# Scores of the second block from the rotated halves: three fp32r passes over 64 rows, in turn of the two row halves

## What is computed

```python
# differential attention: 8 heads, each with two components c of 64 features
q = apply_rope(rms_norm_2(q.reshape(B, S, 8, 2, 64), q_norm), cos, sin)
k = apply_rope(rms_norm_2(k.reshape(B, S, 8, 2, 64), k_norm), cos, sin)
s = einsum('bqhcd,bkhcd->bhcqk', qblk, k) * scale          # causal, query blocks of 128
p = softmax(where(causal, s, NEG_INF))
a = p[:, :, 0] - lam * p[:, :, 1]
o = einsum('bhqk,bkhe->bqhe', a, v)                        # then a norm per head and w_o
# sliding window: 16 query heads of 64 features, 4 key heads, window 128
q = apply_rope(rms_norm_2(q, q_norm), cos, sin)
s = einsum('bnqhgd,bnkhd->bnhgqk', qb, kw) / 8             # 128 queries by 256 keys
m = maximum(max(s), sink); e = exp(s - m)
p = e / (sum(e) + exp(sink - m));  o = einsum('bnhgqk,bnkhd->bnqhgd', p, vw)
```

## Time and profile before

| | |
|---|---|
| median of three runs | 2025.56 us |
| profiled execution: time / span | 2027.33 us / 2025.5 us |
| granted TensorE clock, mean share of full | 0.987 |
| PE busy | 1938.7 us (96%) |
| weight loads (PEld) busy | 1560.5 us (77%) |
| DVE busy | 1222.7 us (60%) |
| ACT busy | 791.4 us (39%) |
| DMAs PR<-TMPR | 144, 128.0 KB by the page |
| DMAs TMP<-TMP | 104 |

### The profile page before, as it was taken

One profiled execution on the slowest core, in us unless ns is written; L12 is line 12 of the kernel. 1 busy time (PEld: TensorE's weight loads), 2 busy tenths in 40 slices (PEclk: granted clock), 3 DMA queues, 4 the chain that ended last, 5 costly groups with the idle time before them and its releaser, 6 DMA issues.

```text
span 2025.5 us, 24525 instructions
## 1 busy us (share of the span) xinstructions
PE 1938.7 (96%) x9230; PEld 1560.5 (77%) x9230; DVE 1222.7 (60%) x2147; ACT 791.4 (39%) x1734; POOL 275.9 (14%) x212
## 2 busy tenths in 40 slices
PE   7999899999999999899979999999989899999999
PEld 5887676788888888666658888888867778888887
DVE  8456986655354466488856535545969875445353
ACT  4444555433232233366643323223357633223231
POOL 3000430111011021011111101101210011101010
PEclk9999999999999999999979999999999999999999
DMA  5232000133323323455423333332353123333322
GB/s 208 70 97 70 1 1 1 53 94 97 102 94 96 102 84 104 116 150 130 119 60 94 102 94 94 103 94 86 104 149 83 27 89 98 94 97 101 94 93 95
DMA packets 62134, 184.41 MB, mean 91 GB/s; under 512 B 9024, under 2 KB 9408, under 8 KB 61760
## 3 DMA queue, kind: packets, MB, share of 16 engines
q1 hardware_dynamic: 62016, 182.83, 30.2%
HBM read 155.01 MB, written 2.10 MB: 78 GB/s over the span
## 4 chain that ended last, share of the span: by engine, by line
PE 77%; DVE 11%; SPq 5%; issue 2%; DMA 2%; ACT 2%; DVEq 0%; ACTq 0%
PE bank L880 22%; PE bank L882 21%; PE bank L881 21%; SPq L792 2%; PE bank L984 2%; DMA TMP<-TMP 2%; SPq L769 2%; PE bank L854 1%; PE bank L1055 1%; PE bank L855 1%; PE bank L856 1%; DVE SM L1654 1%; PE bank L1031 1%; PE bank L1075 1%; DVE WL L1438 1%
## 5 line engine op out<-in xcount | busy, mean ns | idle before, releaser
L1159 ACT ACTIVATE WH<-RAW 128x512 fp32r<-128x512 f32 (+2 forms) x584 | 331.8, 612 | 790.5 <-PE bank L882 725.3
L1438 DVE TENSOR_TENSOR WL<-RAW,WH 128x512 fp32r<-128x512 f32 (+2 forms) x584 | 457.7, 817 | 76.3 <-ACT WH L1159 69.8
L880 PE MATMUL bank<-HH,WH 128*128 128x512 f32 x1056 | 424.7, 402 | 22.5 <-DVE WL L1438 9.9
L880 PE MATMUL bank<-GH,WH 128*128 128x512 f32 x1088 | 435.5, 400 | 7.0 <-DVE GL L1710 4.2
L882 PE MATMUL bank<-GH,WL 128*128 128x512 f32 x1088 | 425.3, 391 | 0.0
L881 PE MATMUL bank<-GL,WH 128*128 128x512 f32 x1088 | 425.0, 391 | 0.0
L882 PE MATMUL bank<-HH,WL 128*128 128x512 f32 x1056 | 413.8, 392 | 0.0
L881 PE MATMUL bank<-HL,WH 128*128 128x512 f32 x1056 | 413.7, 392 | 0.0
L880 PEld LDWEIGHTS bank<-HH,WH 128*128 128x128 f32 x1056 | 200.4, 190 | 69.3 <-DVE WL L1438 9.9
L880 PEld LDWEIGHTS bank<-GH,WH 128*128 128x128 f32 x1088 | 205.8, 189 | 51.2 <-issue 5.9
L882 PEld LDWEIGHTS bank<-GH,WL 128*128 128x128 f32 x1088 | 205.1, 188 | 43.6
(11 more groups left out here) (222 smaller groups left out, 2175.6 us busy)
## 6 DMA issues: line engine op xcount, KB each, us to landing
RAW<-in_wgu SPq DMA_DIRECT2D x132, 512.0 KB, 3.5
RAW<-in_wd SPq DMA_DIRECT2D x48, 512.0 KB, 3.5
PR<-TMPR SPq DMA_DIRECT2D x144, 128.0 KB, 2.3
RAW<-in_wd SPq DMA_DIRECT2D x24, 384.0 KB, 3.1
RAW<-in_da_qk SPq DMA_DIRECT2D x16, 512.0 KB, 3.7
TMP<-TMP SPq DMA_DIRECT2D x104, 64.0 KB, 2.0
RAW<-in_w_inh SPq DMA_DIRECT2D x12, 512.0 KB, 3.5
RAW<-in_w_in SPq DMA_DIRECT2D x8, 512.0 KB, 6.5
```

The lines of the kernel that those rows point to most:

```text
L880: e.matmul(b, w_h, hi[st.x][k], start=(k == 0), stop=False)
L1159: e.activation(whs[s % NW][:, a:b], raw[s % NR][:, a:b], ACT.Copy).then_inc(S["wh"], 1)
L1438: e.tensor_tensor(wls[s % NR][:, a:b], raw[s % NR][:, a:b], whs[s % NW][:, a:b].bitcast(F), ALU.subtract).then_inc(S["wl"], 1)
```

## The change

The stacking DMAs of `qk` and `sq` go (those of `ks` stay, all with eight DMAs, 16 in the two units). The rotated halves are written directly to where the scores read them: queries and keys of differential attention into rings of three buffers `qd`, `kd`, those of `sq` into a ring of two, `qw`. `scores` now makes both components, or both heads of a unit, at once: three passes (high by high, low by high, high by low), each as two matmuls, one over rows 0 to 63 into one bank and one over rows 64 to 127 into another; then the two masks. `rhi` on ACT now waits until the scores that read the buffer are made, which `stk` on SP did before. `qn` and `swp` wait for the rotation by two units back, not for its stacking. The sliding-window steps are numbered anew (`swa`): two heads of a unit in turn per query block, so that an even `sc s n` makes scores n and n+1. In the planner `swp` costs 2400 instead of 1500 and the `stk` of `ks` 4900 instead of 3000.

```diff
+def swa(n):
+    return n // 8 * 2 + n % 2, n // 2 % 4
...
+        old = rope and g >= 2 and (("stk" if 16 <= g - 2 < 18 else "rot"), *ropes[g - 2])
+        o.add("DVE", ("qn", *at), 680, ("rs", *at), st == "in" and ("xcv", 1), old)
...
-        o.add("SP", ("swp", *at), 1500, ("qn", *at), g >= 2 and ("stk", *ropes[g - 2]), lands=1700)
+        o.add("SP", ("swp", *at), 2400, ("qn", *at), old, lands=1900)
         o.add("DVE", ("rot", *at), 1400, ("cs", *at), ("swp", *at))
-        o.add("ACT", ("rhi", *at), 520, ("rot", *at))
+        free = None
+        if st == "qk" and m >= 6:
+            free = ("sc", "d", 4 * (m // 2 - 3) + 3)
+        elif st == "sq" and m >= 2:
+            free = ("sc", "s", 8 * (m - 2) + 6)
+        o.add("ACT", ("rhi", *at), 520, ("rot", *at), free)
         o.add("DVE", ("rlo", *at), 620, ("rhi", *at))
...
-        doubled = st == "ks" or st == "qk" and m % 2
-        o.add("SP", ("stk", *at), 3000 if doubled else 1500, ("rlo", *at), free, lands=1900)
+        if st == "ks":
+            o.add("SP", ("stk", *at), 4900, ("rlo", *at), ("zero",), lands=1900)
...
-            o.add("PE", ("sc", a, i), two * (2 * w // 2 + 90) if a != "n" else 4 * w * 10 // 12 + 500, *after(i),
-                  ("ex", a, i - back) if i >= back else first)
+            if a == "s" and i % 2 == 0:
+                o.add("PE", ("sc", a, i), 3 * (w + 32) * 10 // 24 + 300, *after(i), ("ex", a, i - 2) if i else first)
...
-                e.matmul(b[:, 0:n], lhs, rhs, start=True, stop=False, skip_group_check=True)
-                if rhs_lo is not None:
-                    e.matmul(b[:, 0:n], lhs, rhs_lo, start=False, stop=False, skip_group_check=True)
-                e.matmul(b[:, mcol:n], identb, mask, start=False, stop=True,
-                         skip_group_check=True).then_inc(S["sc"], 1)
+            def scores(s, q, k, mask, mcol, n):
+
+                two = score_bank(s), score_bank(s + 1)
                 p.wait_ge(S["cb"], 16)
+                for t, (x, y) in enumerate(((q[0], k[0]), (q[1], k[0]), (q[0], k[1]))):
+                    for c in range(2):
+                        rows = slice(64 * c, 64 * c + 64)
+                        e.matmul(two[c][:, 0:n], x[rows], y[rows], start=(t == 0), stop=False, skip_group_check=True)
+                for b in two:
+                    e.matmul(b[:, mcol:n], identb, mask, start=False, stop=True,
+                             skip_group_check=True).then_inc(S["sc"], 1)
...
             def rhi(st, m):
                 p.wait_ge(S["nm_q"], NM[st] + m - 6 + 1)
-                e.activation(nat_hi[m % 2], tmp[m % 2], ACT.Copy).then_inc(S["nm_hi"], 1)
+                if st == "qk" and m >= 6:
+                    p.wait_ge(S["sc"], SC["d"] + 8 * (m // 2 - 2))
+                elif st == "sq" and m >= 2:
+                    p.wait_ge(S["sc"], SC["s"] + 8 * (m - 1))
+                e.activation(rotated(st, m)[0], tmp[m % 2], ACT.Copy).then_inc(S["nm_hi"], 1)
```

More of the change, by code:

```diff
@@ L1556, in rlo @@
                 p.wait_ge(S["nm_hi"], g + 1)
[L1557 removed]
+                high, low = rotated(st, m)
+                e.tensor_tensor(low, tmp[m % 2], high.bitcast(F),
                                 ALU.subtract).then_inc(S["nm_lo"], 1)
```

110 lines of the change are left out of this document (48 added, 62 removed).

## The result

The changed kernel takes 1992.87 us (median of 4 runs, 1989.85 to 1995.55); the kernel before 2027.13 (4 runs, 2025.24 to 2029.56). The ratio is 0.9831, 95% interval 0.9814 to 0.9848: 34.3 us faster. The forecast was 2008 with a range of 1995 to 2021.

A forecast was written before the change was run, and what follows sets the result against it. SyncE's queue was taken to lead the chain of waits in differential attention (32.4%). Terms -6.5 - 2 - 7 + 2 + 1 = -12.5 there and -4.5 in the sliding window gave -17 from 2027.33, stated as 2008, range 1995 to 2021.

The forecast's parts named there:

- PE's scores: Both attentions: new pair costs 1.17 us at 512 columns, 0.81 at 128 and 256; charged +2 us and +1.5 us.
- Rival D: Scores on PE: the two row halves stream one behind another, +5 us in total, 2030; chance 0.07.
- The start, -6.5: First scores of differential attention: 3.75 us stack wait, 1.3 of clock and 1.5 of a bank wait go.
- The middle, -2: Differential attention: of VectorE's 16.8 us waits for swaps, 2 us gained, bounds 0 and 8; PE mostly has other work.
- The clock: Differential attention's start: reduced clock after the stall loses 2.6 us at full-speed equivalent, of which 1.3 was counted.
- The end, -7: Last head of differential attention: scores begin earlier without stacking; 7 of 9.4 us taken, bounds 3 and 9.4.
- The sliding window, -4.5: Sliding-window attention: weight load ahead of stacks -3, earlier first scores -3, scores on PE +1.5.
- rival C: The wait only moves: ScalarE's high half waits for late scores, giving most back; 2023, chance 0.10.
- Rival A: VectorE takes SyncE's place as pace-setter in the middle; only -8 us, 2017.5, chance 0.22.
- Rival B: More than forecast: freer queue brings every rotation earlier, PE's mode changes hide; 29.7 us gained, put at 1998, chance 0.16.

The follow-up runs named there:

- The better order alone: The kernel before with only the planner's guesses for swap and stack times corrected, every stack still made: 1998.59 us, ratio 0.986.

## Why the prediction was right and wrong

*PE's scores: right.* A pair with 512 columns between dense passes takes 0.10 to go over (0.33 instead of 0.23 us after the dense pass), 0.99 in the record with masks, and the next dense pass comes 0.09 late: 1.18 against 1.17 forecast. At 256 columns 0.83 to 0.89 against 0.81, at 128 0.77 against 0.81. Long streams on the two row halves do overlap. By the Trainium skill ("TensorEngine Tiling (Array Packing)", Tiling Modes, Key Properties) a change of mode drains TensorE; the trace agrees, with about 0.09 us for each. Rival D is out.

*The start, -6.5: right.* The wait became 0.46 us as forecast. The first scores come 12.6 us earlier, but 26 passes of 512 columns, 5.9 us at 0.2275, now stand behind them instead of ahead, so some 6.7 us are saved. It agrees with PE's idle time up to there, 6.2 before and 0.5 after. The better order alone gives 5.5 of it (71.9 against 77.4, with as many passes ahead).

*The middle, -2: the step that failed.* The prediction had PE with other work in most of VectorE's 16.8 us of waits. In fact PE's transposes wait for softmax weights that VectorE makes behind these rotations. Up to the last pass of the dense block's projection the stage became 17.0 us shorter, and less the start's 6.7 that leaves 10.3 for the middle, where 2 were forecast and another 2 charged for the pairs. PE's idle time in the middle fell from 10.0 to 0.9 us, and the clock, 0.978 there before and 1.000 after, gave about 2.9 (estimate). Both stood in the trace of the kernel before: PE's own idle time in the stretch prices the term, VectorE's waits do not.

*The clock: 1.3 in the sum, at the start alone.* By the estimate it is 8.5 of the 35.4 us between the profiled executions: 6.8 in the dense stage, above all at its end, and 5.1 in the sliding window, less 3.4 in the rest.

*The end, -7: 11.6.* Between the last projection pass and the last head's norm the stage takes 34.9 instead of 46.5 us: 4.9 less idle time, about 4.2 of clock, the rest not assigned. The better order alone gave 4.5 of it.

*The sliding window, -4.5: 9.7.* The mechanism (a weight load ahead of the stacks) was right and mis-sized: 3 was taken for it, and it carries most. PE's idle time up to the first scores fell from 5.7 to 0.1 us with ScalarE's waits for weights, and guesses alone, which move the load, give 9.9. First scores come 10.0 us earlier. Between first scores and end the stage is 0.3 us longer, where 1.5 was charged for the pairs. No wait of ScalarE for scores (rival C) is among its waits in either stretch. Rival A is out too: VectorE is busy 91% of the middle, but PE sets the pace, and more than A's 8 us came.

*What was not priced.* The sum went through the DMAs that the change removes and took the planner's corrected figures as bookkeeping. The old figures let it believe that a swap takes 1.5 + 1.7 us, when it took 3.85 and, behind stacks, up to 8.3 (4.45 late and 3.85), and so it laid 4.0 us of VectorE work between norm and rotation where 5.4 were needed (1.5 late and 3.85). No rival had a term for it. But it is not the one cause of the miss: without any better guess the removal alone gives 28.2 us and a dense stage of 272.7, so the dense block's terms were too small by themselves. The guesses are needed for the sliding window. Rival B came nearest, 1998 forecast against 1992.87 and, for the removal alone, 2000.69. Its mechanism, that every rotation comes earlier, is what happens in the dense stage; its gain in the sliding window needed the guesses, and a free queue for the swaps is not enough by itself (2031.97 with stacks on GpSimd's queue).

What stays open: how the 20 us that better guesses give in the dense stage divide between VectorE's and PE's order, which were only changed together; and why stacks on GpSimd's queue gain nothing, since the scores' waits, the later landings and GpSimd's own order were not taken apart.

## What to carry to other kernels

Where a planner writes out the order, a changed guess is a change of the kernel: price it and test it by itself, by comparing each guess with the trace's duration and asking what work it puts behind the waiting instruction. Test the other part by itself too: here either part alone gave 28 us of 34, and told in one order only, the second looks worthless. Orders of engines fit each other or fail together: half a better order was 11 to 44 us worse than the old one here, so an order is improved by correcting the planner's figures and not by moving one queue's steps. And price a stretch by the bound engine's own idle time and its granted clock there. Those two fell by 34.8 us of the 35.4 gained, while the waits on the side engine that caused them did not tell the size.

## What the hardware showed unexpectedly

- TensorE overlaps matmuls on its two row halves also when all three of one half stand ahead of the three of the other in the program: with 512 columns they start at 0, 0.010, 0.335, 0.345, 0.570 and 0.580 us, almost as with the halves in turn (0, 0.003, 0.335, 0.338, 0.570, 0.573). One behind another at 0.23 us each they would take 1.4 us; the masks follow after 0.91.
- The same transfers within SBUF land after 2.9 us instead of 2.0 once the stacks go through a second queue beside them.
- 128 copies that nobody waits for cost 12.6 us, with swaps behind them in the queue 1.01 us late on average instead of 0.03.
- The mean granted clock is lower in the runs where PE stands still more: 0.991 with 57.4 us idle, 0.987 with 83.7, 0.977 with 114.5 and 0.974 with 111.7. It is no fixed price: 0.996 was seen with 57.2 us idle.
